# Memory heads attended between projection chunks, V chunks in halves between head pairs, causal scores without the masked quarter

## The reference

```python
for layer in range(2):
    mem_k, mem_v = split(mem @ w_mem_kv[layer])           # 4 memory heads of 64, 256 memory rows
    if layer == 0:
        u_b, u_c, u_h, q_mem = split(x @ w_in_a)            # 3 x 768 + 256 columns
        main = u_b * causal_conv3(u_c * u_h)
    else:
        q, q_mem = split(x @ w_q_b); q = rope(q)            # 12 heads of 64
        k, v = split(x_after_layer_0 @ w_kv_shared); k = rope(k)
        main = causal_attention(q, k, v)                    # 256 tokens are one block
    mem_out = softmax(q_mem mem_k^T / 8) mem_v
    x = layer_norm(alpha * x + concat(main, mem_out) @ w_o[layer])
    x = layer_norm(alpha * x + (dense_swiglu(x) if layer == 0 else moe(x)))
```

## Time and profile before

| | before |
|---|---|
| median of 3 runs | 3033.68 us (3032.73 to 3041.62) |
| the profiled execution, its own time | 3038.2 us |
| its span | 3036.4 us |
| TensorE matmuls busy | 2912.0 us (96%) |
| VectorE busy | 2187.7 us (72%) |
| ScalarE busy | 1712.7 us (56%) |
| mean granted TensorE clock | 0.989 |
| DMA over the span | 204 GB/s |

### The profile page before, as it was taken

The page is one execution under the profiler, slowest core; times in us unless marked ns, Lnnn a source line. Parts: engine busy times, 40 slices in busy tenths (PEclk is TensorE's granted clock), DMA queues, the critical chain, the costliest instruction groups (busy, mean ns, idle before and its releaser), DMA issues.

```text
span 3036.4 us, 52018 instructions
## 1 busy us (share of the span) xinstructions
PE 2912.0 (96%) x20799; PEld 2622.4 (86%) x20799; DVE 2187.7 (72%) x2509; ACT 1712.7 (56%) x1984; POOL 205.4 (7%) x146
## 2 busy tenths in 40 slices
PE   7999999999999999999999999998899999999997
PEld 7999998989989999989899989997677887788776
DVE  5769977665567699866555555556588888888887
ACT  4447776344453477763444444443466777667765
POOL 0140113000001501130000000000000000000000
PEclk9999999999999999999999999999899999999999
DMA  7545352546555543525455445553099999999995
GB/s 212 185 160 147 112 153 98 175 148 210 175 173 166 180 128 117 154 99 178 157 192 197 153 153 180 181 187 117 20 366 364 334 351 349 332 333 350 349 333 198
DMA packets 488732, 619.85 MB, mean 204 GB/s; under 512 B 34689, under 2 KB 439059, under 8 KB 488595
## 3 DMA queue, kind: packets, MB, share of 16 engines
q1 hardware_dynamic: 488595, 617.91, 62.1%
HBM read 616.81 MB, written 1.05 MB: 203 GB/s over the span
## 4 chain that ended last, share of the span: by engine, by line
PE 80%; DVE 12%; ACT 4%; issue 2%; DMA 1%; SPq 1%; DVEq 0%; ACTq 0%
PE PS L1112 15%; PE PS L624 12%; PE PS L626 12%; PE PS L625 12%; PE PS L698 11%; DVE w_lo L1676 3%; PE PS L1137 3%; PE PS L1139 3%; PE PS L1138 3%; ACT w_hi L1210 1%; PE PS L1147 1%; PE PS L1094 1%; PE PS L637 1%; PE PS L639 1%; PE PS L1126 1%
## 5 line engine op out<-in xcount | busy, mean ns | idle before, releaser
L1676 DVE TENSOR_TENSOR w_lo<-raw,w_hi 128x2048 fp32r<-128x2048 f32 x313 | 731.9, 2354 | 263.9 <-ACT w_hi L1210 262.9
L624 PE MATMUL PS<-x_hi,w_hi 128*128 128x256 f32 x3200 | 913.2, 285 | 4.9 <-DVE w_lo L1676 4.9
L625 PE MATMUL PS<-x_hi,w_lo 128*128 128x256 f32 x3200 | 907.2, 283 | 0.0
L626 PE MATMUL PS<-x_lo,w_hi 128*128 128x256 f32 x3200 | 907.1, 283 | 0.0
L1210 ACT ACTIVATE w_hi<-raw 128x2048 fp32r<-128x2048 f32 x313 | 598.9, 1913 | 407.1 <-PE PS L698 244.3
L624 PEld LDWEIGHTS PS<-x_hi,w_hi 128*128 128x128 f32 x3200 | 615.8, 192 | 10.8 <-DVE w_lo L1676 5.4
L625 PEld LDWEIGHTS PS<-x_hi,w_lo 128*128 128x128 f32 x3200 | 615.9, 192 | 1.9
L626 PEld LDWEIGHTS PS<-x_lo,w_hi 128*128 128x128 f32 x3200 | 615.6, 192 | 0.0
L1112 PE MATMUL PS<-w_hi,x_hi 128*128 128x512 f32 x704 | 284.8, 404 | 4.9 <-DVE stage L2325 3.8
L1112 PE MATMUL PS<-w_lo,x_hi 128*128 128x512 f32 x704 | 276.5, 393 | 0.0
L1112 PE MATMUL PS<-w_hi,x_lo 128*128 128x512 f32 x704 | 275.5, 391 | 0.0
(11 more groups left out here) (412 smaller groups left out, 4788.0 us busy)
## 6 DMA issues: line engine op xcount, KB each, us to landing
XC<-in_w_gu_moe_dram SPq DMA_DIRECT2D x176, 512.0 KB, 9.4
raw<-in_w_gu_moe_dram SPq DMA_DIRECT2D x132, 512.0 KB, 8.6
raw<-in_w_in_dram SPq DMA_DIRECT2D x64, 1024.0 KB, 5.7
raw<-in_ffn_w_gate_dram SPq DMA_DIRECT2D x44, 1024.0 KB, 5.4
raw<-in_ffn_w_up_dram SPq DMA_DIRECT2D x44, 1024.0 KB, 6.3
raw<-in_ffn_w_down_dram SPq DMA_DIRECT2D x44, 1024.0 KB, 5.1
raw<-in_w_down_moe_dram SPq DMA_DIRECT2D x32, 1024.0 KB, 10.4
G<-in_w_down_moe_dram SPq DMA_DIRECT2D x32, 1024.0 KB, 10.3
```

The source lines that it names most:

```text
L624: mm(dst, w_hi[:, slot, w0:w0 + P], hi, start=start, stop=False, skip_group_check=True)
L625: mm(dst, w_lo[:, slot, w0:w0 + P], hi, start=False, stop=False, skip_group_check=True)
L626: return mm(dst, w_hi[:, slot, w0:w0 + P], lo, start=False, stop=True, skip_group_check=True)
L1676: tt(w_lo[:, slot, :], raw[:, slot, :], w_hi[:, slot, :].bitcast(F32), SUB)\
```

## The change

- **Stage A**: the ten chunks come in the order 9, 3, 6, 0, 4, 7, 1, 5, 8, 2, so the memory queries come first. The scores, turns and outputs of the two memory pairs stand on TensorE after chunks 2, 3, 5, 6 and 7 of that order. The convolution is spread, `gated_taps` at k = 2, 5, 8 and `gated_out` at k = 3, 6, 9. The first two splits for `w_o` stand ahead of the last `convert`. The 15 fillers go. `w_o` is taken in row order 3, 0, 1, 2.
- **Stage B**: order K0 Q0 K1 Q1 K2 Q2 Q3 V0 V1 V2. The swaps come in twos after chunks 2 to 6 and once more later. The V chunks are cut into two halves of 24 matmuls (`v_half`), which stand between the steps of the pairs. Memory pairs go first. The 8 + 5 fillers go.
- **Causal pairs**: for queries 0 to 127 the keys 128 to 255 are left out, so 384 of 512 columns remain for a head in the scores, exponentials, normalisation, turned tiles (6 for 8), copy and outputs. The mask is added on TensorE by four bf16 matmuls (identity by a 128x128 mask) and no longer by VectorE.
- **Places and waits**: turned tiles go into the banks of the pair's own scores, so `scores(p+2)` now waits for the copy of p (before: for the exponentials of p), and VectorE's maximum waits for the scores alone. `probs`, `probs_t`, `tapped` and `att_small` have other addresses. The swaps use the upper halves of banks 6 and 7.
- **SyncE**: the same number of loads, in another order; the mask load shrinks from 256x256 to 128x128.

```diff
+INA_ORDER = [9, 3, 6, 0, 4, 7, 1, 5, 8, 2]
+KVQ_ORDER = [("k", 0), ("q", 0), ("k", 1), ("q", 1), ("k", 2), ("q", 2), ("q", 3), ("v", 0), ("v", 1), ("v", 2)]
+WO_ORDER = [3, 0, 1, 2]
+ROPE_AT = {2: (8, 9), 3: (0, 1), 4: (10, 11), 5: (2, 3), 6: (12, 13)}
+ROPE_LAST = (4, 5)
...
+        ident_bf = sb("ident_bf", [P, P], BF16)
+        mask_bf = sb("mask_bf", [P, P], BF16)
...
+        pairs_a = mem_pairs(0, 18)
+        pairs_b = mem_pairs(1, 6) + [(XC[:, m, :], XC[:, 8 + m, :], v_all, 2 * m, True) for m in range(6)]
+        wo_tiles_a = [(18, 19), (0, 1), (2, 3), (4, 5)]
+        wo_tiles_b = [(6, 7), (0, 1), (2, 3), (4, 5)]
+        parts_of = lambda causal: (slice(0, P), slice(P, P + T)) if causal else (slice(0, T), slice(T, 2 * T))
...
-                sp.dma_start(causal, a["causal"].rearrange("(t p) n -> p t n", p=P)).then_inc(s["params2_in"], 16)
+                sp.dma_start(mask, a["causal"][0:P, 0:P]).then_inc(s["params2_in"], 16)
...
 TensorE
+            def v_half(c, t):
+                bank = 4 + run[0] % 2
+                if t == 0:
+                    if run[1] >= 2:
+                        pe.wait_ge(s["c_evicted"], n.due("c_evicted"))
+                    pe.wait_ge(s["weights_ready"], n.due("weights_ready"))
+                last = row_tile(PS[:, bank, t * T:(t + 1) * T], c % RING, t)
...
+            def scores(pairs, p):
+                q, k, _, _, causal = pairs[p]
+                if p >= 2:
+                    pe.wait_ge(s["att_copied"], n.peek("att_copied"))
+                for t, part in enumerate(parts_of(causal)):
                     for u in range(2):
+                        o = 64 * u
+                        last = mm(PS[:, 2 * (p % 2) + u, part], q[o:o + 64, t * P:(t + 1) * P], k[o:o + 64, 0:part.stop - part.start],
+                                  start=(t == 0), stop=True, skip_group_check=True)
+                if causal:
+                    for u in range(2):
+                        for at in (0, 2 * P):
+                            last = mm(PS[:, 2 * (p % 2) + u, at:at + P], ident_bf[:, :], mask_bf[:, :], start=False, stop=True,
+                                      skip_group_check=True)
...
+            def turn(pairs, p):
+                    places = (0, P, 2 * P) if causal else (0, T, P, T + P)
+                    for i, at in enumerate(places):
+                        last = nc.tensor.transpose(PS[:, 2 * (p % 2) + u, i * P:(i + 1) * P], probs[:, p % 2, u, at:at + P], cst("ident"))
...
-            for i in range(10):
-                c_chunk(B_INA + i, fresh=(i == 0))
-            end_run(waiting=True)
-            pe.wait_ge(s["prm_ready"], n.due("prm_ready"))
-            attention(heads_a, 15)
+            for k in range(10):
+                c_chunk(B_INA + k, fresh=(k == 0))
+                if k == 2:
+                    scores(pairs_a, 0)
+                if k == 3:
+                    scores(pairs_a, 1)
+                if k == 5:
+                    turn(pairs_a, 0)
+                if k == 6:
+                    outputs(pairs_a, 0)
+                    turn(pairs_a, 1)
+                if k == 7:
+                    pe.wait_ge(s["prm_ready"], n.due("prm_ready"))
+                    outputs(pairs_a, 1)
+            end_run()
...
-            end_run(waiting=True)
-            warm(0, 8)
-            swap(rope_at[10])
-            pe.wait_ge(s["roped"], n.due("roped", 2))
-            attention(heads_b, 5)
+            for k in range(7):
+                c_chunk(B_KV + k, fresh=(k == 0))
+                swap(ROPE_AT.get(k, ()))
+            v_half(B_KV + 7, 0)
+            pe.wait_ge(s["c_evicted"], n.peek("c_evicted"))
+            scores(pairs_b, 0)
+            v_half(B_KV + 7, 1)
+            scores(pairs_b, 1)
+            swap(ROPE_LAST)
+            pieces = {0: (8, 0), 1: (8, 1), 3: (9, 0), 4: (9, 1)}
+            for p in range(8):
+                if p:
+                    if p - 1 == 2:
+                        pe.wait_ge(s["c_evicted"], n.peek("c_evicted"))
+                    if p - 1 in (4, 6):
+                        pe.wait_ge(s["c_evicted"], n.due("c_evicted"))
+                    outputs(pairs_b, p - 1)
+                turn(pairs_b, p)
+                if p in pieces:
+                    v_half(B_KV + pieces[p][0], pieces[p][1])
+                if p == 0:
+                    pe.wait_ge(s["roped"], n.due("roped", 2))
+                if p + 2 < 8:
+                    scores(pairs_b, p + 2)
+            outputs(pairs_b, 7)
...
 ScalarE
+            exponent(pairs_b, 0)
+            evict_v(0)
+            exponent(pairs_b, 1)
+            convert((B_KV + 7) % RING)
+            for p in range(8):
+                copy_turned(pairs_b, p)
+                if p:
+                    evict_out(pairs_b, p - 1)
+                if p == 1:
+                    evict_v(1)
+                if p == 4:
+                    evict_v(2)
+                if p + 2 < 8:
+                    exponent(pairs_b, p + 2)
+                if p == 2:
+                    convert((B_KV + 8) % RING)
+                if p == 5:
+                    convert((B_KV + 9) % RING)
+            evict_out(pairs_b, 7)
...
 VectorE
+            for k, i in enumerate(INA_ORDER):
+                if k == 3:
+                    maximum(pairs_a, 0)
+                if k == 4:
+                    normalise(pairs_a, 0)
+                    maximum(pairs_a, 1)
+                if k == 5:
+                    normalise(pairs_a, 1)
+                if k == 9:
+                    dve.wait_ge(s["att_evicted"], n.due("att_evicted", 2))
+                    split_tiles(0, wo_tiles_a, B_WO1)
+                    split_tiles(1, wo_tiles_a, B_WO1)
+                dve.wait_ge(s["c_evicted"], n.due("c_evicted"))
+                if 6 <= i < 9:
+                    gated_taps(i - 6)
+                if i < 3:
+                    gated_out(i)
+                convert((B_INA + k) % RING)
...
+            maximum(pairs_b, 0)
+            normalise(pairs_b, 0)
+            maximum(pairs_b, 1)
+            rope(ROPE_LAST)
+            for p in range(8):
+                if p + 1 < 8:
+                    normalise(pairs_b, p + 1)
+                if p == 1:
+                    convert((B_KV + 7) % RING)
+                if p == 3:
+                    convert((B_KV + 8) % RING)
+                if p == 4:
+                    dve.wait_ge(s["att_evicted"], n.due("att_evicted", 2))
+                    split_tiles(0, wo_tiles_b, B_WO2)
+                if p == 6:
+                    dve.wait_ge(s["att_evicted"], n.due("att_evicted", 2))
+                    split_tiles(1, wo_tiles_b, B_WO2)
+                    convert((B_KV + 9) % RING)
+                if p + 2 < 8:
+                    maximum(pairs_b, p + 2)
```

More of the change, by code:

```diff
@@ L302, in build @@
         rope_cos, rope_sin = rows[:, 0, :], rows[:, 1, :]
-        causal = rows[:, 2:4, :]
+        mask = rows[:, 2, 0:P]
         positions = XC[:, 21, :]
@@ new lines, in turn @@
+            def turn(pairs, p):
+                causal = pairs[p][4]
+                pe.wait_ge(s["att_norm"], n.due("att_norm"))
+                for u in range(2):
+                    places = (0, P, 2 * P) if causal else (0, T, P, T + P)
+                    for i, at in enumerate(places):
+                        last = nc.tensor.transpose(PS[:, 2 * (p % 2) + u, i * P:(i + 1) * P], probs[:, p % 2, u, at:at + P], cst("ident"))
+                last.then_inc(s["att_turned"], n.one("att_turned"))
@@ new lines, in outputs @@
+            def outputs(pairs, p):
+                _, _, vals, head, causal = pairs[p]
+                pe.wait_ge(s["att_copied"], n.due("att_copied"))
+                if p >= 2:
+                    pe.wait_ge(s["att_evicted"], n.due("att_evicted"))
+                for kt in range(2):
+                    tokens = slice(P, T) if causal and kt else slice(0, T)
+                    at = slice(kt * T, kt * T + tokens.stop - tokens.start)
+                    for u in range(2):
+                        col = 64 * (head + u)
+                        last = mm(PS[64 * u:64 * u + 64, 6 + p % 2, tokens], vals[:, kt, col:col + 64], probs_t[:, u, at],
+                                  start=(kt == 0), stop=(kt == 1), skip_group_check=True)
+                last.then_inc(s["att_out"], n.one("att_out"))
@@ new lines, in exponent @@
+            def exponent(pairs, p):
+                b, causal = p % 2, pairs[p][4]
+                act.wait_ge(s["att_max"], n.due("att_max"))
+                for u in range(2):
+                    for t, part in enumerate(parts_of(causal)):
+                        i = 2 * u + t
+                        last = fn(probs[:, b, u, part], PS[:, 2 * b + u, part], ACT.Exp, scale=ATTN_SCALE,
+                                  bias=att_small[:, b, 4 + i:5 + i], accum_out=att_small[:, b, 8 + i:9 + i])
+                last.then_inc(s["att_exp"], n.one("att_exp"))
@@ new lines, in maximum, with normalise @@
```

(23 more changed lines are left out.)

246 lines of the change are left out of this document (82 added, 164 removed).

## The result

The changed kernel takes **3011.86 us** (median of 4 runs, 3010.66 to 3013.34), the kernel before beside it 3035.36 (4 runs); the ratio is 0.9918, 95% interval 0.9906 to 0.993. Four further executions of the changed kernel had a median of 3011.88, nine of the kernel before beside them 3036.26. So the change is worth 23.5 to 24.4 us. The forecast was 3005 us, from a gain of 28.1 us: the sign and the mechanism held, the result lies near the upper end of the range (2998 to 3013), and it is 1 us above the forecast's own range of 3001 to 3011.

The account below looks back on a forecast made before the run. TensorE bounds the kernel, with a serial attention loop making it wait. Gains of 11.1 (A) and 17.0 (B) sum to 28.1 us; from the 3033.7 median that gives 3005.6, said as 3005, own range 3001 to 3011, wider range 2998 to 3013.

Parts of the forecast that it names:

- Stage A: Attention between the projection chunks, no fillers: 18.55 - 5.8 - 1.3 = 11.4 us less, 11.0 with tails; 11.1 taken.
- held up in A: Rival: in stage A a chain of `w_lo` behind maximum and taps reaches TensorE; 3011 to 3013 us, chance 0.06.
- B up to the seventh chunk: Stage B's projections: eight swaps instead of five before that point and two waits, 2.1 us later in all.
- B from there: Stage B, seventh chunk to projection: work 39.7, waits 17.6, half clock 3.3, so 60.6 us; stage B 17.0 us less.
- turn(0): Stage B, first pair's turn: TensorE waits 2.7 us for the normalisation, which ends at 12.1; TensorE is there at 9.4.
- scores(2): Stage B: TensorE waits 2.5 us for pair 0's copy, queued on ScalarE behind exponent(1) and a `w_hi`.
- scores(4): Stage B: no half covers it, so the loop of 4.9 us shows and TensorE waits 2.7 us on the copy.
- I count it at half clock: Stage B from 44 us on: TensorE busy 5.3 of 13.3 us without filler, so half clock adds 3.3 us.
- The causal loop: Stage B's causal pairs: scores 1.0, maximum 1.2, exponentials 1.65, copy 0.84, links 0.2, together 4.9 us where no half covers.
- the dear end: Mask matmuls at the rate of the float32 swaps: 0.86 us instead of 0.30, adding 2.5 us to stage B.
- Clock rivals: TensorE's clock stays full: 3000 us, chance 0.14; or is half through B's pairs: 3020 to 3025 us, chance 0.10.
- The slower case: Rival: half clock from B's first gap through the whole output projection; 12 us slower, 3046 us, chance 0.03.

Follow-up runs that it names:

- the fillers: The changed kernel with 26 filler matmuls of 256 columns added in waits TensorE has anyway in stage B: 3007.02 us.
- the full-width kernel: The changed kernel with the masked quarter computed in the causal pairs, 512 instead of 384 columns and a third mask matmul per head: 3015.73 us.
- the whole reordering: The changed kernel with V halves, V evictions, weight parts and first maximum of stage B in a new order, no work added or removed: 2997.59 us.
- A alone: The kernel before with only stage A's part of the change, stage B as it was: 3026.09 us.

## Why the prediction was right, and where it was not

- **Stage A.** Forecast 11.1 us, measured 10.7. The gap ahead of the projection was put at 1.3 and is 1.29; no chunk waits. The missing 0.4 lies in the attention steps: with what they add to the chunks they take 6.6 us, where I had 5.8, or 6.2 with the tails. A chunk behind such a step takes 5.95 us (1749.40 to 1755.35) and not 5.76. The rival "held up in A" is out.
- **B up to the seventh chunk.** Forecast + 2.1, measured 27.36 - 25.15 = + 2.2 us. The eight swaps and their two waits came as priced.
- **B from there.** Forecast 60.6 us, measured 60.4; but both halves of that sum were off. The waits were forecast as 17.6 us and are 12.4: turn(0) 2.1 (2.7), scores(2) 0.7 (2.5), scores(4) 2.2 (2.7), scores(5) 0.4 (1.5), scores(7) 2.2 (2.7), outputs(6) 4.0 (4.4), outputs(7) 0.9 (1.0). The place of each is right. In their stead TensorE was busy for 47.96 us, where I had 39.7, and 43.0 with the 3.3 for half clock. **The terms that were mis-sized** are these two. First, TensorE's own work: laid off from start to start, some 5.1 us of the 47.96 are half clock, so at full clock it was 42.9 and not 39.7; what a step adds by its tail and to the first matmul behind it I had left out. Second, "I count it at half clock" from 44 us on: the clock fell earlier too, to 0.58 right behind the first wait of 2.1 us and around the wait of scores(4) (0.71 from 2095 to 2099), which makes 3.1 of the 5.1 us. From 44 us on it stayed at 1.00 for ten more microseconds, and half clock came with outputs(6) only: the last three steps make 2.0 us, where I had 3.3. Steps that were longer than I had them took up waits: the copy of pair 0 ended at 18.4 us as I had it, but TensorE was at scores(2) at 17.8 and not at 15.9. So the place of the waits was foreseen, and that the sum came out within 0.2 us is partly luck: a slower step inside a wait costs nothing, and the fillers, which took nearly all half clock away, brought B2 only 1.3 us.
- **The causal loop** of 4.9 us a turn was 5.02 where nothing stood between its steps. **The mask's** four matmuls began 0.33 us ahead of the outputs, forecast 0.30; the dear end, 0.86, is out. Six of them took 0.44 us in the full-width kernel (2107.45 to 2107.89), so one more costs 0.055 us, and 0.11 goes by once for the group.
- **Clock rivals.** It didn't stay full (0.14), and it wasn't half through the pairs: the turns took 0.87 us at full clock in most of B, and the mean was 0.89. The sentence of the Trainium skill (TensorE: Matmul & The Clock Gate, "Part 4: PE-mode transpose") that transposes don't count as busy, by which that rival would have come true, is not borne out as the deciding thing here: each fall in B came with a wait of 2.1 us or more, and fillers in the waits kept the clock, though the wait of 2.17 us ahead of scores(7) was not followed by one. The slower case is out too: 4 us of the projection were at 0.52, as before at 0.57.
- **From the profile to the median.** Most of the error of 6.9 us lies here. The stages gave 27.8 us between two profiles, forecast 28.1, and the profiled execution was to take 3010: two took 3013.3 and 3010.1, with a start of stage A that alone differs by 3.2 us, and the median is 3011.9. That leaves 1.8 us for the working. But I took from one profiled execution and three runs that the median lies 4.5 us lower, and carried that over to a kernel that hadn't run: 4.5 us more, and 0.6 by rounding down. Over 36 executions the kernel before lies only 2.0 us below its profiled one. The other side of this is a gain by medians 3.4 us smaller than by stages, of which 1.4 is B in the kernel before, 104.9 in one profile and 103.5 in another. The rest is open.

## What to carry to other kernels

In a loop over several engines the cost of a step is where it stands in the order of each queue: three weight splits of 1.9 us, moved behind the copies that TensorE waited for (and one low part on VectorE, which could have held up 0.3 us), were worth 8 us of 3012 with no work added or removed, half of it in the code behind, and the whole reordering 14. Before removing a wait, find what is late next; its distance is what you win. And when long waits replace short ones, look at the granted clock behind them, in the stage that follows too.

## What the chip showed that I had not expected

- The time of untouched code changed by up to 5 us (884.2 to 879.2 us behind B) with what stood ahead of it, and the clock at the start is a part of it: 12 matmuls of 512 columns in the first 4 us at 0.52, 19 at 1.00, which makes about 2 us. The kernel with fillers begins at 1.00 too and still has 882.4.
- The length of a wait alone doesn't tell whether the clock falls. In the changed kernel it was 0.58 in the 4 us behind a wait of 2.1 us, while the steps behind another, of 2.17 us, ran at full clock. In the kernel before, 28 us with waits of at most 1.1 us between TensorE's steps (64% busy) ran at 1.00, and then the clock fell to 0.50 with no longer wait ahead of it; in A alone the same steps stayed at 1.00. What decides it no run isolated.
- Single executions reach the same point of block 1, in unchanged code, up to 4 us apart (1732.8 to 1736.9), while in two executions of one program each later stage repeats to 0.1 us. Differences of a few us are better read by stage than by the whole, with the clock column beside them.
